# Passing both parts of a chunk in one kind of product before the other kind, in the slabs read by parts

## The reference

```python
def first_block(x, ...):
    h = x + nsa_mixer(rmsnorm(x, mix_norm_g), ...)        # projections kc, vc, ks, kw, vs, vw, gates, q;
                                                          # 16 heads with three attention branches; w_out
    h = h + swiglu(rmsnorm(h, ffn_norm_g), w_in, w_out)   # (silu(a) * b) @ w_out, 5632 hidden
    return rmsnorm(h, final_norm_g)

def second_block(x, c, ...):
    mod = silu(c) @ w_mod + b_mod                         # 2048 x 12288, one row
    h = rmsnorm(x, g) * (1 + sc1) + sh1
    x = x + g1 * (concat(swa_attention, mla_attention) @ w_out)
    h = rmsnorm(x, g) * (1 + sc2) + sh2
    x = x + g2 * (relu(h @ w_ff1) ** 2 @ w_ff2)           # 8192 hidden
    return rmsnorm(x, final_norm_g)
```

## Time and profile before

| | |
|---|---|
| median of 3 runs | 2104.2 us (2103.86 to 2106.11) |
| span of the profiled execution | 2103.4 us |
| PE busy | 2084.6 us, 99% |
| DVE busy | 1508.8 us, 72% |
| ACT busy | 1059.9 us, 50% |
| read from HBM | 501.79 MB, 240 GB/s over the span |

### The profile page before, as it was taken

The page is one execution under the profiler, slowest core; times in us unless marked ns, Lnnn a source line. Parts: engine busy times, 40 slices in busy tenths (PEclk is TensorE's granted clock), DMA queues, the critical chain, the costliest instruction groups (busy, mean ns, idle before and its releaser), DMA issues.

```text
span 2103.4 us, 29344 instructions
## 1 busy us (share of the span) xinstructions
PE 2084.6 (99%) x11460; PEld 1791.6 (85%) x11460; DVE 1508.8 (72%) x1998; ACT 1059.9 (50%) x1529; POOL 21.8 (1%) x41
## 2 busy tenths in 40 slices
PE   9999999999999999999999999999999999999998
PEld 8888888888888888888888888888888888888887
DVE  6868666788889888988766767577555555556555
ACT  6654555554444434444456666465443444344443
POOL 0000000000000000000000000000000000000000
PEclk9999999999999999999999999999999999999999
DMA  8787334788898999988765525455555555555553
GB/s 333 272 314 281 104 118 162 283 325 323 324 339 325 365 371 346 344 325 336 303 263 172 212 86 189 182 217 194 195 187 196 186 198 188 192 193 187 198 182 121
DMA packets 74968, 506.40 MB, mean 241 GB/s; under 512 B 8730, under 2 KB 9226, under 8 KB 16976
## 3 DMA queue, kind: packets, MB, share of 16 engines
q1 hardware_dynamic: 70992, 488.67, 63.4%
q0 software_dynamic: 3120, 15.07, 1.9%
q10 hardware_dynamic: 720, 0.79, 0.1%
HBM read 501.79 MB, written 2.18 MB: 240 GB/s over the span
## 4 chain that ended last, share of the span: by engine, by line
PE 94%; DVE 3%; ACT 2%; issue 1%; DMA 0%; DVEq 0%; ACTq 0%; SPq 0%
PE region L1163 40%; PE region L1097 30%; PE region L1101 16%; PE region L1152 2%; PE region L1153 1%; ACT m_SP L1623 1%; PE bank L1260 1%; PE bank L1136 1%; DVE m_WLO L1930 1%; PE bank L1219 1%; ACT m_WHI L1543 1%; PE bank L1209 1%; DVE m_SP L2090 1%; PE bank L1273 1%; PE bank L1188 0%
## 5 line engine op out<-in xcount | busy, mean ns | idle before, releaser
L1930 DVE TENSOR_TENSOR m_WLO<-m_RAW,m_WHI 128x1024 fp32r<-128x1024 f32 (+3 forms) x729 | 867.6, 1204 | 476.8 <-ACT m_WHI L1543 451.9
L1543 ACT ACTIVATE m_WHI<-m_RAW 128x1024 fp32r<-128x1024 f32 (+3 forms) x729 | 752.9, 1042 | 655.3 <-PE region L1163 308.9
L1163 PE MATMUL region<-m_WHI,m_HL 128*128 128x512 f32 x1152 | 359.9, 394 | 0.1
L1097 PE MATMUL region<-m_HL,m_WHI 128*128 128x512 f32 x1472 | 357.5, 393 | 0.0
L1097 PE MATMUL region<-m_H,m_WHI 128*128 128x512 f32 x1376 | 328.7, 391 | 0.0
L1097 PEld LDWEIGHTS region<-m_HL,m_WHI 128*128 128x128 f32 x1472 | 269.6, 188 | 52.1 <-issue 0.3
L1097 PEld LDWEIGHTS region<-m_H,m_WHI 128*128 128x128 f32 x1376 | 252.9, 188 | 48.9
L1163 PEld LDWEIGHTS region<-m_WHI,m_HL 128*128 128x128 f32 x1152 | 213.0, 188 | 43.5 <-issue 1.3
L1966 DVE CUSTOM_DVE_ANT_0 m_RAW<-m_RAW,m_CROW,m_consts 128x2048 f32<-128x2048 f32 x96 | 225.1, 2345 | 0.0
L1163 PE MATMUL region<-m_WLO,m_HL 128*128 128x512 f32 x576 | 224.5, 390 | 0.0
L1163 PE MATMUL region<-m_WLO,m_HIDH 128*128 128x512 f32 (+1 forms) x512 | 198.3, 387 | 0.0
(11 more groups left out here) (338 smaller groups left out, 1733.6 us busy)
## 6 DMA issues: line engine op xcount, KB each, us to landing
m_RAW<-in_w_ff SPq DMA_DIRECT2D x124, 1024.0 KB, 4.8
m_RAW<-in_w_mod SPq DMA_DIRECT2D x96, 1024.0 KB, 6.6
m_RAW<-in_ffn_w_in SPq DMA_DIRECT2D x88, 1024.0 KB, 6.0
m_RAW<-in_ffn_w_out SPq DMA_DIRECT2D x44, 1024.0 KB, 6.8
m_RAW<-in_nsa_w_in SPq DMA_DIRECT2D x36, 1024.0 KB, 6.7
m_RAW<-in_nsa_w_out SPq DMA_DIRECT2D x16, 1024.0 KB, 4.9
m_RAW<-in_w_out SPq DMA_DIRECT2D x16, 1024.0 KB, 4.8
m_RAW<-in_w_first SPq DMA_DIRECT2D x8, 1024.0 KB, 5.2
```

The lines of the kernel that those rows point to most:

```text
L1097: mm = e.matmul(region[s["reg"]][:, b, :], hi[:, i, c:c + 128], both[:, k + a + i, :, :].rearrange("p a s -> p (a s)"), start=k + a + i == ...
L1163: mm = e.matmul(o, lhs, rhs, start=start and i == 0, stop=fin and i == 2, skip_group_check=True)
L1543: e.activation(WHI[u % 4][:, 0:(z - a) * ncol], raw[:, a * ncol:z * ncol], ACT.Copy).then_inc(a_hi, 1)
L1930: e.tensor_tensor(WLO[u % 4][:, 0:m], raw[:, a * ncol:z * ncol], WHI[u % 4][:, 0:m].bitcast(F32), ALU.subtract).then_inc(v_lo, 1)
```

## The change

The plan, and so the queues of ACT, DVE, SP and POOL, stay as they are. Within a chunk, PE now passes both parts in one kind and then both in the other: first chunk P0 P1 S0 S1, second chunk S2 S3 P2 P3. `p_part` is raised in the second half of the chunk, once for each part. The waits for `WHI` (`a_hi`) and `WLO` (`v_lo`) move with the calls.

```diff
-        def half_of_part(s, u, a, z, k, turn, fin):
+        def half_of_part(s, n, a, pairs, k, last):
+            u, nk = P.part_of[n, a][0], CHUNKS[n][2]
+            z = a + 4
             tiles = [tile_of(s, k + kk) for kk in range(a, z)]
...
-            pairs = turn == (k + a) // (z - a) % 2
+            second = pairs == (k // 8 % 2 == 1)
             w.wait_ge(a_hi if pairs else v_lo, u + 1)
...
-                    stop = fin and turn == 1 and i == z - a - 1
+                    stop = last and second and i == 3 and z == nk
...
-            if turn == 1:
+            if second:
                 mm.then_inc(p_part, 1)
...
             if s["groups"] is WIDE and s["by_part"]:
-                if (kk - a) % 2:
-                    half_of_part(s, u, a, z, k, (kk - a) // 2, last and z == nk)
+                if kk % 2:
+                    q, odd = kk // 2, k // 8 % 2
+                    half_of_part(s, n, 4 * (q % 2), q // 2 == odd, k, last)
                 return
```

More of the change, by code:

```diff
@@ L1084, in tile_of @@
             return xh, xl
-        def half_of_part(s, u, a, z, k, turn, fin):
+        def half_of_part(s, n, a, pairs, k, last):
+            u, nk = P.part_of[n, a][0], CHUNKS[n][2]
+            z = a + 4
             tiles = [tile_of(s, k + kk) for kk in range(a, z)]
             both = H3 if s["x"] == "h3" else HL
-            hi, lo = [t[:, 0:(z - a) * s["nc"]].rearrange("p (k n) -> p k n", k=z - a) for t in (WHI[u % 4], WLO[u % 4])]
-            pairs = turn == (k + a) // (z - a) % 2
+            hi, lo = [t[:, 0:4 * s["nc"]].rearrange("p (k n) -> p k n", k=4) for t in (WHI[u % 4], WLO[u % 4])]
+            second = pairs == (k // 8 % 2 == 1)
             w.wait_ge(a_hi if pairs else v_lo, u + 1)
```

## The result

The change is slower. Its median is 2118.2 us (2117.5 to 2120.3), that of the kernel before 2104.2 (2103.9 to 2106.1): a ratio of 1.0070, with an interval of 1.0058 to 1.0081. The forecast was +8.4 us; it is +14.0. I got the shares by laying the two traces' PE instructions side by side (there are 11460 in each, in corresponding order) and taking the **drift**, the time of a chunk's start after less that before, both counted from PE's first instruction. Where the drift jumps, time is lost.

The account below looks back on a forecast made before the run. PE was taken as the bound, busy 99% of the span. Terms -1.8 + 1.9 + 1.4 + 0.2 + 5.4 + 1.2 + 0.1 = +8.4 us on 2104.2 gave 2112.6 us (60%), range 2105.5 to 2117.5.

Parts of the forecast that it names:

- qa 3: Attention slab: a transpose wait of 1.5 us where there were 0.3, +1.2 us.
- kw 0: Slab where part 3's low piece would be wanted before it is ready, a new wait of +1.4 us.
- The walk through q3: Slab q3: later buffer releases delay softmax steps and copies in the queues; +1.9 us at scores, another +1.5 at transposes.
- the wait of relu 2: Before part 3's short kind: activations wanted earlier, a wait of 2.3 us instead of 0.4, +1.9 us.
- rival 1: Only operands, no queue: ACT and DVE have slack in attention; about 2106.5 us, chance 17%.
- the q slabs: Attention slabs, later buffer releases: 1.9 + 1.5 - 0.3 (q4) + 2.0 (q5) + 0.3 (q7) = +5.4 us.
- Part 2: Operands wanted earlier in second chunks: relu 2 +1.9, kw 0 +1.4, one glu slab +0.2 us.
- The bound of 8: Upper bound in us for the loss in the attention's q slabs; the lower was 1.9.
- Part 1: Fewer turns between long and short matmuls on PE: 89 slabs x 0.02 us = -1.8 us, bounds 0 to -2.2.
- The 0.2 us forecast for the first glu slab of the second half: There alone among the glu slabs, an operand wanted earlier would come late, by 0.2 us.
- Rival 3: First feed-forward layer: DVE falls behind, about 20 glu slabs wait 0.5 us each; +10 on top, 2122 us, chance 10%.
- The 0.7 us of slack at the tightest slab: Slab glu 10: low piece ready at 654.3, wanted at 655.0 us in the new order, 0.7 us to spare.

Follow-up runs that it names:

- the feed-forward slabs alone: New order only in 71 feed-forward slabs (without relu 2 and the first glu slab of the second half), otherwise the kernel before; 2105.1 us, ratio 1.0001.
- the last one: Kernel before, with the new order only in feed-forward slabs where it had no wait and q-slab splits put behind tile 5; 2102.3 us, ratio 0.9993.
- the late split: Kernel before with its old order; in the q slabs the split four parts ahead is queued behind tile 5 of a chunk; 2102.9 us, ratio 0.9994.
- relu 2 alone: New order only in slab relu 2, everything else as in the kernel before; 2107.4 us, ratio 1.0010.
- q3 alone: New order only in slab q3, the 88 other slabs as in the kernel before; 2107.9 us, ratio 1.0016.

## Why the prediction was right and where it was wrong

**Right: the sign, the places and the mechanism of the queues.** PE's stream sets the end, the steady stretches stayed full, and the waits are at the scores and transposes of q3 and q5, in qa 3, kw 0 and relu 2, ended by the steps that were named. The walk through q3 is good to half a microsecond: scores at 209.8 and 215.7 and the transposes at 220.4 forecast, 210.1, 215.9 and 220.9 measured, less the 2.2 us of drift at the start of q3. kw 0 (+1.4), qa 3 (+1.05 for 1.2) and the wait of relu 2 (2.55 between starts, for 2.3) are as priced. That a queue, not an engine's load, loses the time is shown by the kernel with PE's list unchanged and other queues; rival 1 (only operands) falls with it. Of the 8.0 us that the other queues give back in the q slabs the old order would gain 2.0 as well, so 6.0 of the 8.3 are the later release with what stands behind it, and 2.3 are left.

**The step that failed: there was no term for the clock.** Part 2 priced relu 2 at the change of its wait, +1.9. It cost +3.75: 2.1 of wait and 1.6 of matmuls at half clock behind it, 0.41 for the 8 short ones and 1.16 for the long run. The forecast had looked only at the granted clock of the kernel before, 1.00 everywhere, where no wait behind the first matmuls is longer than 1.5 us of idle time; it took for granted that a wait costs its own length. In q3 the same fall happened and cost nothing, since another engine had the path. Of the change's executions all five had a mean clock of 0.997 or 0.998.

**Mis-sized: the q slabs, +5.4, measured +8.3** with or without a fall of the clock. The walk was right for q3 (3.4 against 3.8) but gave too much back behind it: -0.3 for q4 was +0.1, +2.0 for q5 was 2.8 (its waits of 0.75 and 1.68 us of idle time are each new in full), +0.3 for q7 and what follows was 0.8. And it had nothing for q 1, where PE waits 0.5 us for part 3's low piece, the mechanism of part 2 in a slab that I had not looked at. The bound of 8 was nearly the value; I had taken the middle.

**Part 1: right in size, wrong in its reason.** The 29 relu slabs gave 0.58 us, 0.02 each, and so did the slabs of the first layer. The size is shown, for runs of 16 and 32. The reason given, a price per turn of 0.02 us, is refuted by the kernel that turns 16 times a slab. The Trainium skill, page "TensorE: Matmul & The Clock Gate", section "Back-to-back issue gap", gives for a single isolated matmul a distance that knows only columns, and by it a turn is worth 0 in every order. The trace has 19 ns a turn in long runs and 4 in runs of two, so it is nearer for short runs than for long ones. The 0.2 us forecast for the first glu slab of the second half did not come: the drift goes down by 0.02 us there as in its neighbours.

**Rival 3** did not happen in the change. In other kernels PE did wait for low pieces of that layer, by 0.4 to 1.2 us, in the kernel with the feed-forward slabs alone, in the last one, and once in the one with the late split (silu 2). The three of these waits whose loads are given above stand behind loads that took 6.9 to 7.9 us to land in place of 4.8 or 4.9, not behind a later release; for the others that is open. The 0.7 us of slack at the tightest slab was a number of one execution.

The terms that the forecast lacked, 1.85 in relu 2 and 2.9 in the q slabs, make 4.75 us, about the 4.6 between the forecast +8.4 and the 13.0 of the spans; the medians are another 1.0 apart. That 1.0 is not in the change. Wherever both are on record, an execution's time is 1.7 to 1.9 us more than its span, so the profiled execution of the kernel before, with its span of 2103.4, took about 2105.2 us, 1.0 above its median, while the change's profiled execution is its median.

## What to carry to other kernels

When a change makes an engine release a buffer later, read the queues of the engines that wait for it: every step of a loop that the first engine comes back for, and that stands behind the waiting one, is late by the whole delay, and putting the waiting step behind them is worth more than the order on the engine itself (6.5 us here, with PE's list untouched; about 2 of it the old order gains as well). Price a wait on TensorE by what else it can start: a fall of the clock behind it costs extra only if TensorE is alone on the path behind the wait. And do not count a small gain per slab before the tightest slab's slack has been seen in more than one execution: the same load took 4.8, 4.9 and 7.9 us to land in three of them.

## What the runs showed of the hardware

- The granted clock of TensorE fell from 2.4 to 1.2 GHz behind a wait of 2.4 us of idle time in a stream without gaps, in some executions and not in others of the same kernel: 5 of 11 with relu 2 alone, 4 of 11 with q3 alone, none of 22 with matmuls put into the same waits, none of 11 with the 1.2 us wait of kw 0 (counted by mean clocks of 0.998, which can miss some). It also fell behind three waits of 0.23, 0.77 and 1.70 us close together, and by the mean clocks in 5 of 11 executions of the old order with the late split, whose profile has no wait above 1.70 us in the q slabs.
- With the fall the 8 short matmuls of relu 2 took 1.44 us in place of 1.03, and the run of 32 long ones 8.44 us in place of 7.28.
- A long run of 256-column matmuls, each with its own weights, makes the five 512-column ones behind it slow (233, 236, 228, 232, 231 ns, then 226.7); a run of two makes the two behind it slow by 6 + 6 ns, about half of the 26 ns of the five.
- Loads of 1 MB of weights in the first feed-forward layer took 4.8 to 7.9 us to land, the same load 4.9, 7.9 and 4.8 us in three kernels that issued it at the same place.
